# A key-value product from hi and lo parts, and state updates moved behind the output projection's residual additions

## The chip, the cores and the metric

The kernel runs on one core of a Trainium2 chip. The metric is the device time of one execution in microseconds. TensorE (PE) multiplies, VectorE (DVE), ScalarE (ACT) and GpSimd (POOL) compute on vectors, and SyncE (SP) issues nearly all DMAs. Each engine runs its own stream of instructions in order; semaphores order the streams against each other.

## The reference

One inference step of a two-layer decoder, for a prompt of 16 + 512 tokens and for 8 decode samples of one token: layer 0 mixes tokens by retention, layer 1 by a short gated convolution, each followed by a convolutional gated FFN. All 536 columns (528 prompt tokens and 8 samples) pass the weights together. The change touches the retention layer, cut here to its core (4 heads, dk = 256, dv = 512):

```python
scores = einsum('bhnd,bhmd->bhnm', q, k) * decay_mask
inner  = einsum('bhnm,bhme->bhne', scores, v)
cross  = einsum('bhnd,bhde->bhne', q, s_prev) * cross_decay
k_decay = exp(log_gamma * (L - 1 - n))
kv     = einsum('bhmd,bhme->bhde', k * k_decay, v)
s_new  = exp(log_gamma * L) * s_prev + kv
x = x + (silu(g) * groupnorm(inner + cross)) @ w_out
```

For the prompt, kv is a product over all 528 tokens, whose result is the new state of the prompt. For each of the 8 samples, kv is one outer product of its k (256) and v (512), and its state of 256 x 512 is read from HBM, multiplied by the decay, added to and written back.

## The kernel before, in words

**Layout.** Activations are feature-major: 128 features on the partitions, tokens on the free axis. Weights come from HBM in units of 128 x 1024 (512 KB). SP loads a unit into one of two raw buffers (`load`, L290 to L298). ACT rounds it to fp32r, the hi part (`split_hi`, L846 to L851), DVE subtracts that from the raw unit, the lo part (`split_lo`, L1159 to L1162), into one of four places. A product with weights is then three fp32r matmuls, hi*hi, hi*lo and lo*hi (`three`, L400). A unit is 48 matmuls of some 264 columns. A raw buffer is loaded again after both splits of the unit before last; a unit is split once the unit four places before it has been used.

**A head** of the retention layer takes 16 units: 0 to 3 for Q and K, 4 to 7 for V, 8 to 11 for the gate, 12 to 15 for the output projection. On PE (`head`, L488):
1. Q and K products (units 0, 1, then 2, 3) into PSUM banks 2 to 5 and 0, 1, 6, 7; DVE rotates Q when units 0 and 1 are done and K when units 2 and 3 are (`rotate`, L1274, four products at L1280 and two sums each).
2. V by rows of tokens (units 4 to 7, L514 to L538) into banks 2 to 5. Its first matmul waits for the four products of Q's rotation (L514), which read those banks. V is scaled from PSUM by ACT (blocks 0 and 2, L941) and DVE (blocks 1 and 3, L1331, L1333), in fp32.
3. K is transposed (L548) and scaled by the decay into `k_rows` (ACT, L957); the scores (L565); then the key-value product (L569 to L584): for two halves e of dk and four blocks j of 128 tokens, an fp32 matmul of 512 columns (L575), and for the last 16 tokens a stacked fp32r matmul (L581). The state after the first two blocks is copied out (L972) and used for the later tokens.
4. The inner product with the scores (L593 to L611), the gate (units 8 to 11), group norm and z = silu(g)*o, split into hi and lo (L1004, L1405), and the output projection (L650 to L664), whose unit pairs p = 0 to 3 DVE adds to the residual x (L1437).

**The samples' states.** ACT forms the outer product of sample b as two scaled copies of v, which a DMA has broadcast to all partitions (`outer`, L943 to L951), into one of two halves of the tile `gate`; DVE adds it to the decayed state (`update`, L1350 to L1353). A pair of copies waits for the update before last. In the order that is written out by hand, all eight stand between the splits of units 9 to 13 and the group norm: ACT L977, L980, L982, L986, L987, DVE L1359, L1372, L1376, L1386, L1387. The gate's linear part reuses the tile and waits for all eight (L1408).

**SP's queue** (L328 to L357) is in order: units 0 to 5, the decay table, eight state loads, units 6 to 10, v to HBM and its broadcast back, units 11 to 13, the prompt's kv store, eight state stores, each behind its update, units 14 and 15. After the last head, units of the FFN follow (L366). In the last head ACT and DVE also normalise each new tile of x for the FFN (L1022, L1442), and PE computes the statistic of the norm (`norm_statistic`, L443) in the midst of the FFN's second unit.

Of the kernel before, what the change touches and what calls it, by code (L numbers as in the profile page):

```python
# [36 lines left out]
P = 128  # L37
# [33 lines left out]
X_SETUP = 0  # L71
PAIR_A, PAIR_B = (1, 2), (0, 3)
# [24 lines left out]
def build(nc, io):  # L97
# [8 lines left out]
    with ctx:  # L106
# [32 lines left out]
        with ExitStack() as s2:  # L139
            with ExitStack() as s3:  # L140
                VB = sb("v_bcast", [P, NB, DV], scope=s3)
            ZRH = sb("ret_z_hi", [P, 4, N_RET], F32R, scope=s2)
            ZRL = sb("ret_z_lo", [P, 4, N_RET], F32R, scope=s2)
            S = sb("states", [P, NB, 2 * DV], scope=s2)
            O = sb("q_k_or_out", [P, 4, T], scope=s2)
            Q, K = O[:, 0:2, :], O[:, 2:4, :]
            V = sb("v_rows", [P, 5, DV], scope=s2)
            KN = sb("k_rows", [P, 4, DK], scope=s2)
            KT = sb("k_tail_stack", [P, DK], F32R, scope=s2)
            G = sb("gate", [P, 4 * N_RET], scope=s2)  # L150
            PR = sb("scores", [P, PCOL[4]], scope=s2)
            VS = sb("v_tail_stack", [P, DV], F32R, scope=s2)
# [72 lines left out]
        v_some, sel_ready = sem("v_some"), sem("sel_ready")  # L225
# [29 lines left out]
        def _(pool):  # L255
# [24 lines left out]

            pool.memset(VS[:].bitcast(F32), 0.0).then_inc(vs_zero, 1)  # L281

# [5 lines left out]
        def _(sp):  # L288
# [39 lines left out]
            def head(h, first):  # L328
                for n in range(4 if first else 0, 6):
                    in_heads(h, n)  # L330
                if first:
                    sp.wait_ge(ss_sum, 7)
                else:
                    sp.wait_ge(s_upd, NB * h)
                sp.dma_start(DEC[:], io["decay"][h]).then_inc(dec_in, 16)
                for b in range(NB):
                    if not first:
                        sp.wait_ge(s_out[b], 16 * h)
                    sp.dma_start(S[:, b, :], st_in[b, h]).then_inc(s_in[b], 16)
# [5 lines left out]
                sp.wait_ge(v_sent, 16 * h + 16)  # L345
                for half in range(2):
                    b = half * NB // 2
                    sp.dma_start(VB[:, b:b + NB // 2, :], VSCR[b:b + NB // 2, :].partition_broadcast(P)).then_inc(vb_in[half], 16)
# [4 lines left out]
                for b in range(NB):  # L353
                    sp.wait_ge(s_upd, NB * h + (b + 1))
                    sp.dma_start(st_out[b, h], S[:, b, :]).then_inc(s_out[b], 16)
                for n in range(14, 16):
                    in_heads(h, n)  # L357

            for h in range(HEADS):
                head(h, h == 0)  # L360
# [5 lines left out]
            def ffn_units(l):  # L366
                with sp.Fori(0, JF // 2) as i:
# [28 lines left out]
        def _(pe):  # L396
# [91 lines left out]
            def head(h, first, last):  # L488
# [54 lines left out]
                for j, (m0, mn) in enumerate(BLK):  # L543
                    for e in range(2):
                        at = (j % 2) * DK + e * P
                        if j == 4 and e == 0:
                            pe.wait_ge(v_some, 2 * h + 1)
# [5 lines left out]
                for j, (m0, mn) in enumerate(BLK):  # L553
                    if j == 0:
                        pe.wait_ge(v_ready, 3 * h + 2)
                        pe.wait_ge(v_some, 2 * h + 1)
                    elif j == 1:
                        pe.wait_ge(v_ready, 3 * h + 3)
                    elif j == 2:
                        pe.wait_ge(v_some, 2 * h + 2)  # L560
# [8 lines left out]
                pe.wait_ge(kn_ready, 4 * h + 4)  # L569
                for js in ((0, 1), (2, 3, 4)):  # L570
                    for e in range(2):
                        if js[0] == 2:
                            pe.wait_ge(mid_ready, 2 * h + e + 1)
                        for j in js[:2]:
                            out = mm(PS[:, 6 + e, :], KN[:, j, e * P:(e + 1) * P], V[:, j, :], start=j in (0, 2), stop=j == 1)  # L575
# [264 lines left out]
        def _(act):  # L840
# [73 lines left out]

            def head(h, first, last):
# [23 lines left out]
                for b in (0, 2):  # L939
                    act.wait_ge(v_acc, 3 * h + b + 1)  # L940
                    fn(V[:, b, :], PS[:, 2 + b, :], ACT.Copy, scale=RN[:, b:b + 1]).then_inc(v_ready, 1)  # L941

                def outer(b):  # L943

                    if b in (0, NB // 2):
                        act.wait_ge(vb_in[b // (NB // 2)], 16 * h + 16)
                    if b >= 2:
                        act.wait_ge(s_upd, 8 * h + (b - 1))
                    for e in range(2):
                        at = (b % 2) * 1024 + e * DV  # L950
                        fn(G[:, at:at + DV], VB[:, b, :], ACT.Copy, scale=KD8[:, e, b:b + 1]).then_inc(samp_kv, 1)  # L951

                act.wait_ge(dec_in, 16 * h + 16)
                act.wait_ge(knat_done, 2 * h + 1)
                for j in range(4):
                    src = PS[:, (6, 6, 7, 7)[j], (j % 2) * DK:(j % 2 + 1) * DK]
                    fn(KN[:, j, :], src, ACT.Copy, scale=DEC[:, DEC_ROW + j:DEC_ROW + j + 1]).then_inc(kn_ready, 1)  # L957
# [5 lines left out]
                act.wait_ge(vs_zero, 1)  # L963
# [5 lines left out]
                split_hi(5 + NS, U_HEAD, h)  # L969
# [3 lines left out]
                fn(OS[:], PS[:, 1, :], ACT.Copy).then_inc(os_ready, 1)  # L973
                split_hi(6 + NS, U_HEAD, h)
                if first:
                    act.wait_ge(prep_step, 12)
                outer(0)  # L977
                split_hi(7 + NS, U_HEAD, h)

                outer(1)  # L980
                for dt in range(4):
                    outer(dt + 2)  # L982
# [3 lines left out]
                outer(6)  # L986
                outer(7)  # L987
# [41 lines left out]
            for b in range(NB):  # L1029
                act.wait_ge(s_out[b], 16 * HEADS)  # L1030

            def ffn(l, norm_no):
# [3 lines left out]
                def body(i, first):  # L1036
                    split_hi(u0 + NS, 4, i)
                    if first:
                        act.wait_ge(stat_done, norm_no + 1)
                        root(3, n_in // 2, halves(R[:, c0:]), rstd)  # L1040
                    split_hi(u0 + 1 + NS, 4, i)
# [12 lines left out]
                    split_hi(u0 + 3 + NS, 4, i)  # L1054
                    for t in range(2):
# [99 lines left out]
        def _(dve):  # L1155
# [116 lines left out]

            def head(h, first, last):
# [52 lines left out]
                dve.wait_ge(v_ready, 3 * h + 1)  # L1326
# [3 lines left out]
                dve.wait_ge(v_acc, 3 * h + 2)  # L1330
                ts(V[:, 1, :], PS[:, 3, :], RN[:, 1:2], None, ALU.mult).then_inc(v_some, 1)  # L1331
                dve.wait_ge(unit_done, U_HEAD * h + (NS + 8))
                ts(V[:, 3, :], PS[:, 5, :], RN[:, 3:4], None, ALU.mult).then_inc(v_some, 1)  # L1333

                dve.wait_ge(score_done, 3 * h + 1)
                tt(PR[:, C_RET:PCOL[1]], PS[:, 2, C_RET:CUT], DEC[:, C_RET:CUT], ALU.mult).then_inc(p_ready, 1)
                dve.wait_ge(score_done, 3 * h + 2)
# [12 lines left out]
                def update(b):  # L1350
                    dve.wait_ge(samp_kv, 16 * h + (2 * b + 2))
                    at = (b % 2) * 1024
                    stt(S[:, b, :], S[:, b, :], DEC[:, DEC_STATE:DEC_STATE + 1], G[:, at:at + 1024], ALU.mult, ALU.add).then_inc(s_upd, 1)  # L1353

# [4 lines left out]
                update(0)  # L1359
                split_lo(NS + 7, U_HEAD, h)  # L1360
# [11 lines left out]
                for b in range(1, 5):  # L1372
                    update(b)
                for dt in range(1, 4):
                    channel_sum(dt)
                update(5)  # L1376
# [9 lines left out]
                update(6)  # L1386
                update(7)  # L1387
# [20 lines left out]
                dve.wait_ge(s_upd, NB * h + NB)  # L1408
# [24 lines left out]
                for p in range(4):  # L1433
# [15 lines left out]
            def ffn(l, norm_no):  # L1449
# [306 lines left out]
```

## Time and profile before

| what | value |
|---|---|
| median of 3 runs | 1459.53 us (1459.17 to 1459.82) |
| time of the profiled execution | 1459.5 us |
| its span, first to last instruction | 1457.7 us |
| granted TensorE clock, mean | 1.000 |
| HBM read, written | 149.39 MB, 21.55 MB |

The span in 40 slices of some 36 us; a digit is the busy share of a slice in tenths:

```profile
PE   9999999999999999999999999999999999999998
DVE  7785577468458855555552327444565555553222
ACT  5552273264155633333331324222343333332222
```

The heads are the first twelve to thirteen slices (a head is 121 us), the FFN of layer 0, the convolution layer and the second FFN follow. A busy engine in such a line has an instruction running; it may still be waited for by nobody. Matmuls are pipelined and their ends are modelled, so intervals between the starts of successive matmuls say what one costs.

### The profile page before, as it was taken

To read this page: it belongs to the slowest core of one execution; us is meant where nothing else is said; L and a number is where in the kernel's file an instruction comes from. 1 tells how busy PE (TensorE), PEld (TensorE's weight loads), DVE (VectorE), ACT (ScalarE), POOL (GpSimd) and SP (SyncE) were. 2 spreads that over 40 slices of the span, in tenths; PEclk is the share of its full clock that TensorE was granted. 3 is DMA by queue.
4 is the path that set the end of the run, shared out by engine and by line. 5 is a ranking of instruction groups with operands and counts; after the bars stand their busy time and mean duration, and the time that the engine had idled before them with its cause. 6 is when DMAs were issued, how large, how long until landed. Compare 5 with 4: busy or idle time off the path is not lost.

```text
span 1457.7 us, 27410 instructions
## 1 busy us (share of the span) xinstructions
PE 1451.0 (100%) x11460; PEld 1396.8 (96%) x11460; DVE 798.6 (55%) x1063; ACT 543.5 (37%) x776; POOL 3.4 (0%) x25
## 2 busy tenths in 40 slices
PE   9999999999999999999999999999999999999998
PEld 8699789879969999999999999999999999999998
DVE  7785577468458855555552327444565555553222
ACT  5552273264155633333331324222343333332222
POOL 0000000000000000000000000000000000000000
PEclk9999999999999999999999999999999999999999
DMA  8445253463444322222222222223222222223221
GB/s 300 147 187 183 102 214 118 170 228 108 177 155 184 102 93 96 86 86 96 91 90 88 100 88 87 87 89 101 89 87 98 89 86 95 92 86 99 94 87 59
DMA packets 47743, 171.91 MB, mean 118 GB/s; under 512 B 5608, under 2 KB 6248, under 8 KB 46624
## 3 DMA queue, kind: packets, MB, share of 16 engines
q1 hardware_dynamic: 47488, 170.71, 33.7%
q8 instruction: 63, 1.03, 0.3%
q14 instruction: 16, 0.13, 0.0%
q0 software_dynamic: 32, 0.03, 0.0%
q10 hardware_dynamic: 144, 0.00, 0.0%
HBM read 149.39 MB, written 21.55 MB: 117 GB/s over the span
## 4 chain that ended last, share of the span: by engine, by line
issue 100%; POOL 0%; POOLq 0%
POOLq L106 0%; POOL v_tail_stack L281 0%; POOL ident L266 0%; POOL k_tail_stack L275 0%; POOL h_tail L263 0%; POOL mean_v L259 0%; POOL ident L257 0%; POOL h_lo L262 0%; POOL h_hi L261 0%; POOL sample_ones L274 0%; POOL mean_d L258 0%; POOL scores_end_stack L277 0%; POOL late_q_decayed L276 0%; POOL sample_ones L279 0%; POOL seed L268 0%
## 5 line engine op out<-in xcount | busy, mean ns | idle before, releaser
L851 ACT ACTIVATE w_hi<-w_raw 128x1024 fp32r<-128x1024 f32 x227 | 240.0, 1059 | 669.1 <-PE ps L406 469.9
L406 PE MATMUL ps<-h_hi,w_hi 128*128 128x264 f32 (+2 forms) x2300 | 468.3, 285 | 1.5 <-DVE h_lo L1190 1.5
L406 PE MATMUL ps<-h_lo,w_hi 128*128 128x264 f32 (+2 forms) x2300 | 465.3, 284 | 0.0
L406 PE MATMUL ps<-h_hi,w_lo 128*128 128x264 f32 (+2 forms) x2300 | 465.0, 283 | 0.0
L1162 DVE TENSOR_TENSOR w_lo<-w_raw,w_hi 128x1024 fp32r<-128x1024 f32 x227 | 277.1, 1223 | 332.1 <-ACT w_hi L851 331.8
L406 PEld LDWEIGHTS ps<-h_hi,w_hi 128*128 128x128 f32 x2300 | 355.8, 188 | 2.8 <-issue 2.1
L406 PEld LDWEIGHTS ps<-h_hi,w_lo 128*128 128x128 f32 x2300 | 355.5, 188 | 0.0
L406 PEld LDWEIGHTS ps<-h_lo,w_hi 128*128 128x128 f32 x2300 | 355.2, 188 | 0.0
L700 PE MATMUL ps<-z_hi,w_hi 128*128 128x264 f32 (+1 forms) x704 | 144.6, 283 | 0.0
L700 PE MATMUL ps<-z_hi,w_lo 128*128 128x264 f32 (+1 forms) x704 | 144.6, 283 | 0.0
L700 PE MATMUL ps<-z_lo,w_hi 128*128 128x264 f32 (+1 forms) x704 | 144.5, 283 | 0.0
L700 PEld LDWEIGHTS ps<-z_lo,w_hi 128*128 128x128 f32 x704 | 109.9, 188 | 0.0
L700 PEld LDWEIGHTS ps<-z_hi,w_lo 128*128 128x128 f32 x704 | 109.8, 188 | 0.0
L700 PEld LDWEIGHTS ps<-z_hi,w_hi 128*128 128x128 f32 x704 | 109.8, 188 | 0.0
L1484 DVE TENSOR_TENSOR tmp<-ps,rms 128x524 f32<-128x524 f32 (+1 forms) x44 | 28.8, 697 | 76.1 <-PE ps L406 76.1
L1465 DVE TENSOR_TENSOR tmp<-ps,rms 128x528 f32<-128x528 f32 (+1 forms) x44 | 29.0, 701 | 68.9 <-PE ps L406 68.9
L532 PE MATMUL ps<-w_hi,h_hi 128*128 128x512 f32 x128 | 52.2, 408 | 0.0
L406 PE MATMUL ps<-ret_z_hi,w_hi 128*128 128x264 f32 x256 | 52.0, 284 | 0.0
L406 PE MATMUL ps<-ret_z_lo,w_hi 128*128 128x264 f32 x256 | 51.9, 284 | 0.0
L406 PE MATMUL ps<-ret_z_hi,w_lo 128*128 128x264 f32 x256 | 51.8, 284 | 0.0
L532 PE MATMUL ps<-w_hi,h_lo 128*128 128x512 f32 x128 | 50.5, 395 | 0.0
L532 PE MATMUL ps<-w_lo,h_hi 128*128 128x512 f32 x128 | 50.5, 394 | 0.0
(208 smaller groups left out, 1413.7 us busy)
## 6 DMA issues: line engine op xcount, KB each, us to landing
w_raw<-in_w_units_dram SPq DMA_DIRECT2D x227, 512.0 KB, 3.2
states<-in_state_ret_dram SPq DMA_DIRECT2D x32, 512.0 KB, 9.0
out_ret_s_dram<-states SPq DMA_DIRECT2D x32, 512.0 KB, 4.7
v_bcast<-v_scratch SPq DMA_DIRECT2D x8, 1024.0 KB, 5.7
x_res<-in_x_all_dram SPq DMA_DIRECT2D x8, 268.0 KB, 6.1
out_ret_p_dram<-tmp SPq DMA_DIRECT2D x4, 512.0 KB, 3.8
out_y_prompt_dram<-y_rows SPq DMA_DIRECT2D x4, 512.0 KB, 2.6
decay<-in_decay_dram SPq DMA_DIRECT2D x4, 287.0 KB, 3.9
```

The source lines that it names most:

```text
L406: out = mm(PS[:, 2 * s + half, at:at + n_col], a, b[:, lo:lo + n_col], start=first and n == 0, stop=last and n == 2)
L532: out = mm(PS[:, 2 + b, :], a, c, start=k == 0 and q == 0, stop=k == KD - 1 and q == 2)
L700: out = mm(PS[:, 2 * DOWN[t] + half, to:to + n_col], a, z[:, j, lo:lo + n_col], start=j == 0 and q == 0, stop=j == JF - 1 and q == 2)
L851: fn(WH[:, c % NS, :], RAW[:, c % NR, :], ACT.Copy).then_inc(hi_ready, 1)
L1162: tt(WL[:, c % NS, :], RAW[:, c % NR, :], WH[:, c % NS, :].bitcast(F32), ALU.subtract).then_inc(lo_ready, 1)
L1465: tt(halves(TMP[:, t, 0:n_in]), slot(PAIR_A[t], w), halves(R[:, c0:]), ALU.mult).then_inc(up_read, 1)
L1484: tt(halves(TMP[:, t, 4:n_in]), slot(PAIR_B[t], n_out // 2), halves(R[:, c0 + 4:]), ALU.mult).then_inc(gate_read, 1)
```

## The change

**Products.** `k_rows` becomes two fp32r tiles, hi and lo, and V gets a hi and a lo tile beside its fp32 one. ACT writes all four blocks of V and their hi parts and K's hi part, DVE the lo parts. Each of the eight products of a head is three fp32r matmuls in place of an fp32 one. The stacked matmuls and all other products stay.

**Outer products and updates** leave the middle of the head. In heads 1 to 3 samples 0, 1 follow pair 1 of the output projection's additions, 2, 3 follow pair 2, 4 to 7 follow pair 3. In the last head 0, 1 follow pair 0 with its norm tiles, 2, 3 pair 1, and 4 to 7 stand in the first body of the FFN, behind the root (ACT) and the reciprocal (DVE).

**SP** loads V's broadcast only when the inner product is done, since the tile that takes it now lies over V, the scores and the value stack; the next head's (or the FFN's) units 0 and 1 come ahead of the stores, 2 and 3 between them; in a head after the first, state loads 0 to 3 come ahead of units 4 and 5. POOL clears the value stack once a head, after the last update of the head before.

The diff, cut to its core:

```diff
+UPDATES = (((), (0, 1), (2, 3), (4, 5, 6, 7)), ((0, 1), (2, 3), (), ()))
...
-                VB = sb("v_bcast", [P, NB, DV], scope=s3)
+                VH = sb("v_rows_hi", [P, 4, DV], F32R, scope=s3)
+                VL = sb("v_rows_lo", [P, 4, DV], F32R, scope=s3)
...
+            with ExitStack() as s7:
+                KNH = sb("k_rows_hi", [P, 4, DK], F32R, scope=s7)
+                KNL = sb("k_rows_lo", [P, 4, DK], F32R, scope=s7)
...
-            pool.memset(VS[:].bitcast(F32), 0.0).then_inc(vs_zero, 1)
+            for h in range(HEADS):
+                if h > 0:
+                    pool.wait_ge(samp_kv, 16 * h)
+                pool.memset(VS[:].bitcast(F32), 0.0).then_inc(vs_zero, 1)
...
+            def head(h, first, last):
+                if not first:
+                    for b in range(4):
+                        load_state(b)
+                for n in range(4, 6):
                     in_heads(h, n)
...
+                for b in range(0 if first else 4, NB):
+                    load_state(b)
                 for n in range(6, 11):
                     in_heads(h, n)
...
                 sp.wait_ge(kv_ready, h + 1)
                 sp.dma_start(kv_dst[h], KV).then_inc(kv_sent, 16)
-                for b in range(NB):
-                    sp.wait_ge(s_upd, NB * h + (b + 1))
-                    sp.dma_start(st_out[b, h], S[:, b, :]).then_inc(s_out[b], 16)
+                sp.wait_ge(v_sent, 16 * h + 16)
+                sp.wait_ge(inner_done, 4 * h + 4)
+                for half in range(2):
+                    b = half * NB // 2
+                    sp.dma_start(VB[:, b:b + NB // 2, :], VSCR[b:b + NB // 2, :].partition_broadcast(P)).then_inc(vb_in[half], 16)
                 for n in range(14, 16):
                     in_heads(h, n)
+                for n in range(2):
+                    next_unit(h, n)
+                for p in range(4):
+                    for b in UPDATES[last][p]:
+                        store_state(h, b)
+                    if p in (1, 2):
+                        next_unit(h, 1 + p)
+                if last:
+                    ffn_in_unit(0, 1, 0)
+                    for b in range(4, NB):
+                        store_state(h, b)
...
-                pe.wait_ge(kn_ready, 4 * h + 4)
...
+                            pe.wait_ge(kn_lo, 4 * h + 2 * e + 2)
+                            pe.wait_ge(v_lo, 4 * h + 4)
                         for j in js[:2]:
-                            out = mm(PS[:, 6 + e, :], KN[:, j, e * P:(e + 1) * P], V[:, j, :], start=j in (0, 2), stop=j == 1)
+                            kh, kl = KNH[:, j, e * P:(e + 1) * P], KNL[:, j, e * P:(e + 1) * P]
+                            for q, (k, v) in enumerate(((kh, VH), (kh, VL), (kl, VH))):
+                                out = mm(PS[:, 6 + e, :], k, v[:, j, :], start=j in (0, 2) and q == 0, stop=j == 1 and q == 2)
...
                 for p in range(4):
                     if not (last and p == 3):
                         split_hi(12 + p + NS, U_HEAD, h)
+                    for b in UPDATES[last][p]:
+                        outer(h, b)
                     if last:
...
                         root(3, n_in // 2, halves(R[:, c0:]), rstd)
+                    if first and l == 0:
+                        for b in range(4, NB):
+                            outer(HEADS - 1, b)
...
-                ts(V[:, 1, :], PS[:, 3, :], RN[:, 1:2], None, ALU.mult).then_inc(v_some, 1)
...
+                for b in range(4):
...
+                    tt(VL[:, b, :], V[:, b, :], VH[:, b, :].bitcast(F32), ALU.subtract).then_inc(v_lo, 1)
...
                     if last:
                         for k in (2 * p, 2 * p + 1):
                             norm_tile(k, 1, C_RET, N_RET, D_FFN)
+                    for b in UPDATES[last][p]:
+                        update(h, b)
...
                         dve.wait_ge(r_ready, norm_no + 1)
+                        if l == 0:
+                            for b in range(4, NB):
+                                update(HEADS - 1, b)
```

ACT's order in the middle changes with it: the split of unit 9 now follows the copies of the middle state (L972), and DVE's split of unit 11 follows the kv sum (L1371).

## Rows read from the trace of the kernel before

**Rows 1.** The page, busy us (share of the span) xinstructions

```profile
PE 1451.0 (100%) x11460; PEld 1396.8 (96%) x11460; DVE 798.6 (55%) x1063; ACT 543.5 (37%) x776; POOL 3.4 (0%) x25
```

**Rows 2.** The waits, TensorE: waited for, us in total, times, longest us

```profile
PE ps L406 <- DVE h_lo L1190: 1.5, 3, 0.7
```

**Rows 3.** Timeline, TensorE, third head: start us, us to last end, instruction, count

```profile
302.31 0.40 PE L532 MATMUL ps<-w_hi,h_lo 128*128 128x512 f32 x1
302.55 0.39 PE L532 MATMUL ps<-w_lo,h_hi 128*128 128x512 f32 x1
302.77 1.25 PE L548 MATMUL ps<-ident,q_k_or_out 128*128 128x128 f32 x10
...
306.86 5.42 PE L575 MATMUL ps<-v_rows,k_rows 128*128 128x512 f32 x12
311.71 0.79 PE L581 MATMUL ps<-v_tail_stack,k_tail_stack 96*128 96x512 f32 x1
312.35 1.88 PE L575 MATMUL ps<-v_rows,k_rows 128*128 128x512 f32 x4
...
314.30 0.80 PE L603 MATMUL ps<-scores,v_rows 128*128 128x248 f32 x4
```

**Rows 4.** Timeline, ScalarE, third head, in brackets the idle time before it

```profile
301.58 0.69 ACT L941 ACTIVATE v_rows<-ps,rms_rows 128x512 f32<-128x512 f32 x1 [2.10 <-PE ps L532]
303.91 1.57 ACT L957 ACTIVATE k_rows<-ps,decay 128x256 f32<-128x256 f32 x4 [1.64 <-PE ps L548]
...
312.52 1.33 ACT L951 ACTIVATE gate<-v_bcast,dec_k 128x512 f32<-128x512 f32 x2
```

**Rows 5.** Groups by line, whole span: xcount, busy us, mean ns, idle before

```profile
L851 ACT ACTIVATE w_hi<-w_raw 128x1024 fp32r<-128x1024 f32 x227 | 240.0, 1059 | 669.1 <-PE ps L406 469.9
L1162 DVE TENSOR_TENSOR w_lo<-w_raw,w_hi 128x1024 fp32r<-128x1024 f32 x227 | 277.1, 1223 | 332.1 <-ACT w_hi L851 331.8
L1353 DVE SCALAR_TENSOR_TENSOR states<-states,decay,gate 128x1024 f32<-128x1024 f32 x32 | 40.3, 1280 | 2.6 <-ACT gate L951 2.6
```

**Rows 6.** Timeline, third head, where the output projection starts

```profile
348.80 0.70 DVE L1405 TENSOR_TENSOR ret_z_lo<-q_k_or_out,ret_z_hi 128x528 fp32r<-128x528 f32 x1
...
349.94 0.40 PE L406 MATMUL ps<-ret_z_hi,w_hi 128*128 128x264 f32 x2
```

**Rows 7.** Timeline, last head: rotation of Q, start of the value product

```profile
387.35 0.70 DVE L1280 SCALAR_TENSOR_TENSOR q_k_or_out<-ps,cos_r 128x528 f32<-128x528 f32 x1
...
389.19 0.70 DVE L1280 SCALAR_TENSOR_TENSOR tmp<-ps,cos_r 128x528 f32<-128x528 f32 x1
...
396.76 0.39 PE L532 MATMUL ps<-w_hi,h_hi 128*128 128x512 f32 x1
```

**Rows 8.** State loads; landings of those issued at 376.8 and 380.9; weight loads

```profile
376.83 4.49 SPq L339 DMA_DIRECT2D states<-in_state_ret_dram  x8
...
DMA to landing us min/median/max: 5.7/5.7/5.7
...
DMA to landing us min/median/max: 11.2/11.2/11.2
...
w_raw<-in_w_units_dram SPq DMA_DIRECT2D x227, 512.0 KB, 3.2
```

**Rows 9.** Timeline, last head into the FFN

```profile
492.23 1.22 DVE L1162 TENSOR_TENSOR w_lo<-w_raw,w_hi 128x1024 fp32r<-128x1024 f32 x1
...
494.33 0.41 PE L406 MATMUL ps<-h_hi,w_hi 128*128 128x264 f32 x2
...
499.69 0.71 DVE L1175 TENSOR_TENSOR tmp<-tmp 128x528 f32<-128x528 f32 x1
...
501.63 1.05 PE L439 MATMUL ps<-tmp,mean_d 128*128 128x264 f32 x4
```

**Rows 10.** Stretches at the start: us, TensorE busy (x), clock, DMA share, GB/s

```profile
1.30:4.30 3.00, 3.00 (x14) 1.00 0.74 230
4.40:5.40 1.00, 1.00 (x11) 1.00 0.71 168
```

More of the change, by code:

```diff
@@ L326, in _, with ffn_in_unit, next_unit, store_state @@
             sp.dma_start(CF[:], io["ffn_consts"]).then_inc(ffn_in, 16)
-            def head(h, first):
-                for n in range(4 if first else 0, 6):
+            def ffn_in_unit(l, i, n):
+                load(U_FFN_IN[l] + 4 * i + n)
+            def next_unit(h, n):
+                if h < HEADS - 1:
+                    in_heads(h + 1, n)
+                else:
+                    ffn_in_unit(0, 0, n)
+            def store_state(h, b):
+                sp.wait_ge(s_upd, NB * h + (b + 1))
+                sp.dma_start(st_out[b, h], S[:, b, :]).then_inc(s_out[b], 16)
+            def head(h, first, last):
+                def load_state(b):
+                    if not first:
+                        sp.wait_ge(s_out[b], 16 * h)
+                    sp.dma_start(S[:, b, :], st_in[b, h]).then_inc(s_in[b], 16)
+                if not first:
+                    for b in range(4):
+                        load_state(b)
+                for n in range(4, 6):
                     in_heads(h, n)
@@ L344, in head @@
                 sp.dma_start(VSCR, V[16:24, 4, :]).then_inc(v_sent, 16)
[L345 to L348, printed above, removed]
                 for n in range(11, 14):
@@ L352, in head @@
                 sp.dma_start(kv_dst[h], KV).then_inc(kv_sent, 16)
[L353 to L355 removed]
+                sp.wait_ge(v_sent, 16 * h + 16)
[3 more added lines that the diff above has]
+                    sp.dma_start(VB[:, b:b + NB // 2, :], VSCR[b:b + NB // 2, :].partition_broadcast(P)).then_inc(vb_in[half], 16)
                 for n in range(14, 16):
                     in_heads(h, n)
+                for n in range(2):
[9 more added lines that the diff above has]
+                        store_state(h, b)
             for h in range(HEADS):
[L360 removed]
+                head(h, h == 0, h == HEADS - 1)
             for l in range(2):
@@ L366, in ffn_units @@
             def ffn_units(l):
-                with sp.Fori(0, JF // 2) as i:
+                if l == 1:
+                    for n in range(4):
+                        ffn_in_unit(l, 0, n)
+                for n in range(1 if l == 0 else 0, 4):
+                    ffn_in_unit(l, 1, n)
+                with sp.Fori(2, JF // 2) as i:
                     for n in range(4):
@@ L913, in _, with outer @@
             fn(RN[:], PS[:, 3, 300:305], ACT.Sqrt, bias=EPST[:]).then_inc(rows_rstd, 2)
+            def outer(h, b):
+                if b == 0:
+                    act.wait_ge(z_mul, 8 * h + 8)
+                if b in (0, NB // 2):
+                    act.wait_ge(vb_in[b // (NB // 2)], 16 * h + 16)
+                if b >= 2:
+                    act.wait_ge(s_upd, 8 * h + (b - 1))
+                for e in range(2):
+                    at = (b % 2) * 1024 + e * DV
+                    fn(G[:, at:at + DV], VB[:, b, :], ACT.Copy, scale=KD8[:, e, b:b + 1]).then_inc(samp_kv, 1)
             def head(h, first, last):
@@ L938, in head @@
                 fn(VT, PS[:, 0, 0:P], ACT.Copy, scale=RN[:, 4:5]).then_inc(v_ready, 1)
-                for b in (0, 2):
-                    act.wait_ge(v_acc, 3 * h + b + 1)
-                    fn(V[:, b, :], PS[:, 2 + b, :], ACT.Copy, scale=RN[:, b:b + 1]).then_inc(v_ready, 1)
[L943 to L951, printed above, removed]
+                for b in range(4):
+                    if b < 3:
+                        act.wait_ge(v_acc, 3 * h + b + 1)
+                    else:
+                        act.wait_ge(unit_done, U_HEAD * h + (NS + 8))
+                    fn(V[:, b, :], PS[:, 2 + b, :], ACT.Copy, scale=RN[:, b:b + 1]).then_inc(v_ready, 1)
+                    fn(VH[:, b, :], PS[:, 2 + b, :], ACT.Copy, scale=RN[:, b:b + 1]).then_inc(v_hi, 1)
                 act.wait_ge(dec_in, 16 * h + 16)
+                if first:
+                    act.wait_ge(prep_step, 12)
                 act.wait_ge(knat_done, 2 * h + 1)
@@ L973, in head @@
                 fn(OS[:], PS[:, 1, :], ACT.Copy).then_inc(os_ready, 1)
+                split_hi(5 + NS, U_HEAD, h)
                 split_hi(6 + NS, U_HEAD, h)
-                if first:
-                    act.wait_ge(prep_step, 12)
-                outer(0)
                 split_hi(7 + NS, U_HEAD, h)
-                outer(1)
                 for dt in range(4):
-                    outer(dt + 2)
                     act.wait_ge(inner_done, 4 * h + (dt + 1))
@@ L1054, in body @@
                     split_hi(u0 + 3 + NS, 4, i)
+                    if first and l == 0:
+                        for b in range(NB):
+                            act.wait_ge(s_out[b], 16 * HEADS)
                     for t in range(2):
@@ L1271, in first_scale, with update @@
                         tt(t[:, e, c:], t[:, e, c:], R[:, c:], ALU.mult).then_inc(qk_scaled, 1)
+            def update(h, b):
+                dve.wait_ge(samp_kv, 16 * h + (2 * b + 2))
+                at = (b % 2) * 1024
+                stt(S[:, b, :], S[:, b, :], DEC[:, DEC_STATE:DEC_STATE + 1], G[:, at:at + 1024], ALU.mult, ALU.add).then_inc(s_upd, 1)
             def head(h, first, last):
@@ L1371, in head @@
                 tt(KV, PS[:, 6:8, :].rearrange("p e v -> p (e v)"), KM, ALU.add).then_inc(kv_ready, 1)
-                for b in range(1, 5):
-                    update(b)
+                split_lo(NS + 7, U_HEAD, h)
                 for dt in range(1, 4):
                     channel_sum(dt)
-                update(5)
                 dve.wait_ge(gstat_done, 2 * h + 1)
```

62 lines of the change are left out of this document (26 added, 36 removed).

## The prediction

> **What bounds the kernel now.** I read the busy line first: TensorE is busy for 1451.0 of 1457.7 us, VectorE for 798.6, ScalarE for 543.5 [rows 1]. Then the waits: beside one before the very first matmuls, the only wait of TensorE is 1.5 us at the start [rows 2]. So the kernel is a TensorE stream with no holes. A change can gain only what it takes out of that stream, and every wait that it opens is lost in full. The averages of the other engines don't say whether one opens; that is decided in the stages, followed below with the third head (297 to 397 us) as pattern.
>
> **The products.** Two fp32r matmuls of 512 columns start 0.23 us apart (302.31, 302.55, 302.77). The old key-value block runs from 306.86 to 314.30: 16 fp32 records and two stacked ones [rows 3]. That is 7.44 us; with 0.23 for each stacked one, an fp32 record costs (7.44 - 0.46)/16 = 0.436, a product two of them, 0.87. The new product is three fp32r matmuls, 0.69. A head has eight products: 24 x 0.23 + 0.46 = 5.98, and with some 0.1 for the change of operand 6.1. Gain: 1.3 us a head, 5.3 us in all. Bounds: nothing, if fp32r ran no faster here, and 5.8 without the 0.1.
>
> **The split of V and K** is covered. ScalarE now makes eight copies of 512 columns where it made two (0.69 each, some 0.6 apart), each pair as its block finishes every 1.4 us. The last pair starts at 303.0 and ends at 304.3; the four key copies, 1.57 us, end at 305.8 instead of 305.5 [rows 4]. VectorE loses two copies and gets four differences of V (0.7 each, like the residuals of [rows 6]) and four of K (0.5, an estimate from 256 of 512 columns): V's last rest is there at 305.1, K's first two at 306.0, the others, behind one score product, at 307.2. TensorE has ten transposes and the scores until 306.86 and takes the second pair at 308.25, so nothing waits; the nearest margin is 0.9 us. The score products come about 0.5 us later and hold up only the copies of the middle state, needed at 309.6 and there at 309.2. If that cover were gone, 0.5 us a head would be lost. The clearing of the value stack on POOL is off every path: POOL is idle and the stack is next used some 40 us later, with the next head's V.
>
> **Updates out of the middle.** In the third head the first rest of z is finished at 349.50, TensorE starts the output projection at 349.94 [rows 6]: 0.4 us of room. The 1.3 us gained would mostly be lost there if nothing moved. Without six updates (1.28 us each) and eight outer pairs (1.33 us) [rows 4, 5] ahead of it, this chain ends about 3 us earlier. The gain survives, and TensorE starts at 348.6.
>
> **Updates behind the residual additions, heads 1 to 3.** TensorE takes 5.85 us a weight unit (46.8 us from 349.94 to 396.76 for eight) [rows 6, 7]. So projection pair 1 ends at 360.3, and the value product of the next head should start at 395.4. Call the next head's weight units N0 to N5. SyncE issues in order: N2 stands behind the stores of states 0 and 1, N3 behind 2 and 3; N4 and N5, until now loaded before any state, stand behind stores 4 to 7 **and** four state loads. The chain:
> - 360.5 N1 is split on ScalarE (1.06), two outer pairs (2.6), second update (1.3): 365.5.
> - Store, N2 issued 366.0, landed 369.3 (3.2) [rows 8], split on ScalarE 370.4, two pairs 373.0, fourth update 374.3.
> - Store, N3 issued 374.8, landed 378.1, ScalarE 379.2, VectorE (1.22) 380.5.
> - Updates 4 to 7: 1.3 each, plus a wait for the buffer of two (a pair needs the update before last): 386.0.
> - Store, four state loads half a microsecond apart (eight in 4.49), N4 issued at 388.4, N5 at 388.8.
> - Landing: the first state load of the old burst took 5.7 us, the eighth, issued 4.0 later, 11.2: they land in turn, (380.9 + 11.2 - 376.8 - 5.7)/7 = 1.37 apart [rows 8]. The first of four at 386.4 + 3.2 = 389.6, so N4 at 395.1 and N5 at 396.5.
> - N5 on ScalarE 397.6, on VectorE 398.8; both are written before the rotation of Q, whose fourth product comes 2.54 us later [rows 7]: 401.4.
> TensorE may not overwrite the banks before that: 401.4 - 395.4 = **6.0 us of stall**. Before, that product was there at 389.89, 6.9 us early. It happens at three boundaries: 18.0 us. Bounds: 2.4 each if N4 and N5 do not queue behind the states (below), 7.5 if the burst starts as slowly as the old one (5.7 instead of 3.2).
>
> **Last head.** There the same engines also normalise the new tiles. Times from the start of the projection (before: 494.33 - 23.4 = 470.9). VectorE: additions of pair 0 to 10.3, split to 11.5, norm of two tiles (held back by the outer pairs on ScalarE) to 15.8, two updates to 18.1, additions of pair 1 to 19.4. TensorE wants these at 17.5: stall 1.9. Split 20.6, norm 23.4, updates 25.8, additions of pair 2 27.0; wanted at 25.3: stall 1.7. FFN unit 2 now stands behind store 3: issued 26.3, landed 29.5, split on both engines 31.9. From there the old kernel took from 493.45 to 500.40, 6.95 us, to the last sum of squares; its statistic ran at 501.63, 1.2 us later [rows 9]. New: 38.9, wanted at 501.63 - 470.9 + 3.6 = 34.3, stall 4.6. Sum **8.2 us**. Bounds: 3.7 (four updates, 4.9, less the 1.2 of room) and 10. The last four updates, behind the reciprocal, end at about 51; the banks that they hold back are wanted at 56. They and the FFN loads behind their stores cost nothing; without that cover they would cost up to 5.
>
> **Clock.** The only start of TensorE from rest in this trace: 14 matmuls of 128 columns in 3.0 us, later 11 in 1.0 [rows 10], though the column of the granted clock says 1.00 for both; the spacing is that of 1.2 and then 2.4 GHz. Those 14 cost about 1.4 us more than later ones. Whether a hole of 6 us brings this back no row shows: nothing at the least, 2.8 at the most (twice as many). I take 1.4 for each of the three, because the row after a rest is the nearest: 4.2 us.
> The Trainium skill's page "TensorE: Matmul & The Clock Gate" (Part 1) says that the array falls to half clock when it has been idle. By that rule the three stalls cost the 4.2 us; without it the sum is 1480.4.
>
> **Sum**, against the profiled execution's 1459.5 us (span 1457.7, 1.8 around it; the median of the runs is 1459.53, the same): 1459.5 - 5.3 + 18.0 + 8.2 + 4.2 = **1484.6 us**. Measurement tells some 0.2%, 2.9 us, from no change.
>
> **Rivals.**
> - No drop of the clock, all else as above: 1480.4. For it: a hole is not the start of a kernel. Chance 0.2.
> - The weight loads overtake the states. N4 and N5 would land at 391.6 and 392.0, the rotation's fourth product be there at 397.8, a stall of 2.4 each and no drop of the clock: 1459.5 - 5.3 + 7.2 + 8.2 = 1469.6. Against it: the old state loads land one after another. Chance 0.1.
>   The Trainium skill's page "DMA: Bandwidth & Descriptors" (Queues, rings and completion order) states that completion isn't first-in first-out per issuing engine, which is this rival's rule.
> - Faster: all moved updates are hidden, and the gain stays: 1454.2. The one mechanism is the slack of the rotation of Q, 6.9 us before. It decides at N5's landing: by 390.4 (395.4 less the 5.0 of splits and rotation) TensorE would see nothing. For it: VectorE is only half busy. Against: the chain needs 388.8 for the mere issue, and the last head has 1.2 us of room for 4.9 us of work. Chance 0.1.
> - The products don't get faster (three fp32r cost what two records of fp32 do): 1489.9. Against: [rows 3]. Chance 0.03.
>
> **Chances and range.** My forecast has 0.5; 0.07 is left for what I haven't seen, most of it slower. Range 1465 to 1494: the lower end takes in the overtaking loads with a cheap last head, the upper three stalls of 7.5 and the dearer clock. Faster 0.1, the same 0.04, slower 0.86.
>
> **What would show it.** Waits of TensorE before the first 512-column product of heads 2 to 4, about 6 us, ended by the rotation (L1280), its VectorE idle until a split that ScalarE started on a landing weight; matmuls after it at twice the spacing; three smaller waits in the last projection and at the first FFN statistic. Key-value records 0.23 us apart, the block 6.1 us long. z's rests earlier than the projection by 2 us. If no wait stands before the value product, the chain on SyncE is wrong; if it is 2.4, the queueing is; if the key-value block still takes 7.4 us, the gain is.

## The result, and the profile after

The changed kernel takes **1498.93 us** (median of 4 runs, 1498.53 to 1499.47) beside 1459.55 us of the kernel before (1459.17 to 1459.82): a ratio of 1.0271, 95% interval 1.0258 to 1.0283. That is 39.4 us slower where 25.1 were forecast, and above the range. The profiled execution has a span of 1497.5 us. Of the executions reported below, one of the ten of experiment 7 took 5309.54 us at a granted clock of 1.0; nothing on record explains it, and no ratio here contains it.

First the page of the changed kernel, busy time by engine and the row of slices of TensorE (PEclk is its granted clock, in tenths):

```profile
PE 1455.8 (97%) x11492; PEld 1409.4 (94%) x11492; DVE 809.5 (54%) x1087; ACT 557.5 (37%) x800; POOL 5.0 (0%) x28
...
PE   9999799799979989999999999999999999999998
...
PEclk9999899999999999999999999999999999999999
```

The full stream of [rows 1] now has places below 9: three between the heads and one in the last head. Then the waits of TensorE (waited for: us in total, times, longest us):

```profile
PE ps L574 <- DVE tmp L1332: 25.6, 3, 10.1
PE ps L481 <- DVE tmp L1222: 4.5, 1, 4.5
PE ps L448 <- DVE x_res L1489: 3.2, 2, 1.8
...
PE ps L448 <- DVE h_lo L1215: 1.1, 1, 1.1
```

[Rows 2] held 1.5 us there. L574 is the value product of heads 2 to 4, L1332 the rotation of Q, L481 the first FFN statistic, L1489 the residual additions of the last head, L1215 the lo part of a tile that is normalised for the FFN.

**The products** in the third head (timeline of TensorE: start us, us, instruction, count):

```profile
326.88 0.50 PE L616 MATMUL ps<-v_rows_hi,k_rows_hi 128*128 128x512 f32 x1
327.21 0.39 PE L616 MATMUL ps<-v_rows_lo,k_rows_hi 128*128 128x512 f32 x1
...
333.05 0.58 PE L644 MATMUL ps<-scores,v_rows 128*128 128x248 f32 x2
```

The block takes 333.05 - 326.88 = 6.17 us instead of the 7.44 of [rows 3], one product every 0.23. By the starts of the stages the four heads save 1.26 to 1.27 each, 5.05 in all.

**The split** is there in time. ScalarE (first row) and VectorE in the same head:

```profile
324.15 1.57 ACT L1006 ACTIVATE k_rows_hi<-ps,decay 128x256 fp32r<-128x256 f32 x4
```

```profile
325.02 0.88 DVE L1391 SCALAR_TENSOR_TENSOR k_rows_lo<-ps,decay,k_rows_hi 128x256 fp32r<-128x256 f32 x2
...
326.14 0.87 DVE L1391 SCALAR_TENSOR_TENSOR k_rows_lo<-ps,decay,k_rows_hi 128x256 fp32r<-128x256 f32 x2
```

The first pair of rests is finished at 325.9, a microsecond ahead of the product; the second at 327.0, wanted some 1.4 us after 326.88. **The chain of z** gained what was forecast: its first rest ends at 366.5 and the output projection starts at 368.69, 2.2 us of room instead of the 0.4 of [rows 6]:

```profile
365.79 0.70 DVE L1458 TENSOR_TENSOR ret_z_lo<-q_k_or_out,ret_z_hi 128x528 fp32r<-128x528 f32 x1
```

**The holes.** The queue of SyncE between the second and third head (projection from 238.82), behind the stores of states 0 and 1 at 254.35 and 255.55; then landings of single weight loads, of N2 (255.99), N3 (265.27) and N4 (280.08) here, and of N3 one boundary earlier:

```profile
255.99 0.40 SPq L307 DMA_DIRECT2D w_raw<-in_w_units_dram  x1
263.61 1.56 SPq L348 DMA_DIRECT2D out_ret_s_dram<-states  x2
265.27 0.41 SPq L307 DMA_DIRECT2D w_raw<-in_w_units_dram  x1
273.32 4.25 SPq L348 DMA_DIRECT2D out_ret_s_dram<-states  x4
277.62 2.37 SPq L354 DMA_DIRECT2D states<-in_state_ret_dram  x4
280.08 0.98 SPq L307 DMA_DIRECT2D w_raw<-in_w_units_dram  x2
...
DMA to landing us min/median/max: 3.9/3.9/3.9
...
DMA to landing us min/median/max: 4.3/4.3/4.3
...
DMA to landing us min/median/max: 7.4/7.4/7.4
...
DMA to landing us min/median/max: 5.4/5.4/5.4
```

What waited for it, on ScalarE, VectorE and TensorE:

```profile
287.57 1.06 ACT L892 ACTIVATE w_hi<-w_raw 128x1024 fp32r<-128x1024 f32 x1 [11.67 <-DMA w_raw<-in_w_units_dram]
```

```profile
288.66 2.50 DVE L1209 TENSOR_TENSOR w_lo<-w_raw,w_hi 128x1024 fp32r<-128x1024 f32 x2 [11.44 <-ACT w_hi L892]
291.07 0.70 DVE L1332 SCALAR_TENSOR_TENSOR q_k_or_out<-ps,cos_r 128x528 f32<-128x528 f32 x1
...
292.92 0.70 DVE L1332 SCALAR_TENSOR_TENSOR tmp<-ps,cos_r 128x528 f32<-128x528 f32 x1
```

```profile
285.40 0.41 PE L448 MATMUL ps<-h_hi,w_lo 128*128 128x268 f32 x2
293.67 0.80 PE L574 MATMUL ps<-w_hi,h_hi 128*128 128x512 f32 x1 [7.86 <-DVE tmp L1332]
294.26 0.63 PE L574 MATMUL ps<-w_hi,h_lo 128*128 128x512 f32 x1
294.69 0.63 PE L574 MATMUL ps<-w_lo,h_hi 128*128 128x512 f32 x1
```

ScalarE stood idle for 11.7 us (the number in brackets) until N4 had landed, VectorE for 11.4 until ScalarE had split it: neither was short of time. TensorE starts the value product 10.2, 8.0 and 7.9 us late at the three boundaries, by the starts of the stages.

**The clock.** Behind the hole the products stand 0.43 us apart and not 0.23. Four stretches, two in the wait and two behind it (us, TensorE busy (x), weight loads, VectorE, ScalarE, POOL, granted clock, DMA share, GB/s):

```profile
285.30:291.00 5.70, 0.51 (x5) 0.29 (x3) 2.29 (x2) 2.11 (x2) 0.00 (x0) 1.00 1.03 411
291.00:293.60 2.60, 0.00 (x0) 0.00 (x0) 2.60 (x5) 0.00 (x0) 0.00 (x0) 0.51 1.01 400
...
293.70:297.70 4.00, 4.00 (x10) 3.13 (x11) 3.93 (x7) 0.00 (x0) 0.00 (x0) 0.50 0.01 4
298.10:302.10 4.00, 4.00 (x31) 2.65 (x29) 3.10 (x7) 2.56 (x4) 0.00 (x0) 1.00 0.13 20
```

The clock is at its lower level, 1.2 GHz, already at the end of the wait; it makes the three value products longer by 2.15, 2.03 and 2.02 us. The same rows show the DMA engines full (share 1.03 and 1.01, 411 and 400 GB/s) all through the wait: N4 and N5 landed in the midst of a burst, four state loads ahead of them and four behind.

**The last head**: the projection becomes 3.56 us longer, and from the FFN's first product to steady work 8.55 more are lost, 1.1 and 4.5 of them waits (above), the rest, 2.9, at half clock.

| term, us | forecast | measured |
|---|---|---|
| products | -5.3 | -5.05 |
| three holes | 18.0 | 26.1 |
| last head, waits | 8.2 | 9.2 |
| clock | 4.2 | 9.1 |
| sum | 25.1 | 39.35 |

### The profile page after: what moved, and what is told of

It reads as the page before. It is cut to its first block, busy times and chain, and to the rows that moved or that the text cites. A ratio compares the mean times of both kernels' runs of the same rounds, so it can differ in the third digit from the quotient of the medians.

```text
span 1497.5 us, 27488 instructions
## 1 busy us (share of the span) xinstructions
PE 1455.8 (97%) x11492; PEld 1409.4 (94%) x11492; DVE 809.5 (54%) x1087; ACT 557.5 (37%) x800; POOL 5.0 (0%) x28
## 3 DMA queue, kind: packets, MB, share of 16 engines
q8 instruction: 63, 1.03, 0.3%
## 4 chain that ended last, share of the span: by engine, by line
issue 73%; PE 19%; DMA 3%; DVE 3%; ACT 1%; SPq 1%; POOLq 0%; POOL 0%; ACTq 0%
PE ps L448 8%; PE ps L574 5%; DMA w_raw<-in_w_units_dram 3%; DVE states L1323 2%; PE ps L616 1%; DVE w_lo L1209 1%; PE ps L647 1%; ACT w_hi L892 1%; PE ps L602 1%; PE ps L644 1%; PE ps L649 1%; PE ps L481 0%; PE ps L544 0%; PE ps L553 0%; ACT gate L966 0%
## 5 line engine op out<-in xcount | busy, mean ns | idle before, releaser
L574 PE MATMUL ps<-w_hi,h_hi 128*128 128x512 f32 x128 | 55.2, 432 | 25.6 <-DVE tmp L1332 25.6
L574 PEld LDWEIGHTS ps<-w_hi,h_hi 128*128 128x128 f32 x128 | 25.6, 200 | 34.7 <-DVE tmp L1332 26.3
L574 PE MATMUL ps<-w_hi,h_lo 128*128 128x512 f32 x128 | 52.6, 411 | 0.0
L574 PE MATMUL ps<-w_lo,h_hi 128*128 128x512 f32 x128 | 52.6, 411 | 0.0
```

What stands on the lines that cost most here:

```text
L574: out = mm(PS[:, 2 + b, :], a, c, start=k == 0 and q == 0, stop=k == KD - 1 and q == 2)
```

## The experiments

The theory after the result: **the order of SyncE's queue** makes the holes (weight loads stand behind state stores, which stand behind updates), and each hole costs clock on top. Its rivals: the updates' own work on ScalarE and VectorE, or slow transfers.

**1. Weight loads ahead of the stores, heads 1 to 3.**

```diff
                 for p in range(4):
+                    if not last:
+                        next_unit(h, 2 + p)
                     for b in UPDATES[last][p]:
                         store_state(h, b)
-                    if p in (1, 2):
+                    if last and p in (1, 2):
                         next_unit(h, 1 + p)
...
                 if not first:
                     for b in range(4):
                         load_state(b)
-                for n in range(4, 6):
-                    in_heads(h, n)
+                else:
+                    for n in range(4, 6):
+                        in_heads(h, n)
```

> Edit: in heads 1 to 3 SyncE issues each weight load of the next head (N2 to N5) ahead of the state stores that it stood behind, and N4 and N5 ahead of the four state loads; no work of any engine and no byte changes, and the last head stays as it is. Theory Q (the loads stand in SyncE's order behind stores that wait for updates): the three holes before the value products (10.2, 8.0, 7.9 us, sum 26.1) go, and with them the slow value matmuls behind them (6.2 us in all): 1498.9 - 32.3 = 1466.6 us, with the last head's stalls unchanged. Rival W (the updates' own work on ScalarE and VectorE is too much at that place): the rotation of Q stays late by the updates' 1.3 us each, holes of 3 us or more stay, 1476 us or more. Rival B (the transfers are slow because stores and loads share the DMA engines): holes of 2 to 4 us stay.

Measured: 1467.44 us (1466.92 to 1467.65), ratio to before 1.0054 (1.0037 to 1.0071). The waits of TensorE hold no value product any more:

```profile
PE ps L484 <- DVE tmp L1225: 4.5, 1, 4.5
PE ps L451 <- DVE x_res L1492: 3.1, 2, 1.8
```

VectorE at the same place in front of the fourth head, whose value product starts at 393.19:

```profile
376.15 1.29 DVE L1326 SCALAR_TENSOR_TENSOR states<-states,decay,gate 128x1024 f32<-128x1024 f32 x1
...
382.63 1.23 DVE L1212 TENSOR_TENSOR w_lo<-w_raw,w_hi 128x1024 fp32r<-128x1024 f32 x1 [4.05 <-ACT w_hi L895]
383.77 0.70 DVE L1335 SCALAR_TENSOR_TENSOR q_k_or_out<-ps,cos_r 128x528 f32<-128x528 f32 x1
...
385.62 0.70 DVE L1335 SCALAR_TENSOR_TENSOR tmp<-ps,cos_r 128x528 f32<-128x528 f32 x1
```

All eight updates are done at 377.4 and the rotation is 6.9 us early, as it was before the change. No instruction of ScalarE, VectorE or TensorE differs: 31.5 us are the order of one queue (and the clock that the holes cost). The rival of the work falls for these heads. That of slow transfers falls as a cause of its own: issued early, N4 and N5 land 3.3 and 3.4 us after their issue (from 366.57 and 372.40). But where these loads come late, transfers that share the full DMA engines are a part of the hole: N4 took 4.9 us behind the stores (experiment 2), and 7.4 behind four state loads as well (the changed kernel).

**2. Only N4 and N5 ahead of the state loads**

```diff
-                if not first:
-                    for b in range(4):
-                        load_state(b)
                 for n in range(4, 6):
                     in_heads(h, n)
+                if not first:
+                    for b in range(4):
+                        load_state(b)
```

> Edit: in heads 1 to 3 only N4 and N5 are issued ahead of the four state loads of the next head; they still stand behind the eight stores, as N2 and N3 do. Theory Q: N4 is issued some 2 us earlier and lands 4 us behind its issue instead of 7.4, so each hole shrinks by 5 us, from 8 to about 3 (the first to 5): 1498.9 - 15 = 1484 us, and up to 6 less (1478) if TensorE's clock doesn't fall after so short a hole. Rival W (work of the updates): the order of these loads decides nothing, 1499. Rival B (shared DMA engines): N4 and N5 still take 7 us behind the stores, 1495 or more.

**3. Only N2 and N3 ahead of the stores**

```diff
                 for p in range(4):
+                    if not last and p < 2:
+                        next_unit(h, 2 + p)
                     for b in UPDATES[last][p]:
                         store_state(h, b)
-                    if p in (1, 2):
+                    if last and p in (1, 2):
                         next_unit(h, 1 + p)
```

> Edit: in heads 1 to 3 only N2 and N3 are issued ahead of the stores; N4 and N5 stay behind the stores and the four state loads. Theory: the updates then end 7.3 us earlier (31.1 us behind the projection's start, by the trace of the run with all four ahead, instead of 38.4), so N4 and N5 land that much earlier and the holes shrink from 8 to about 1, too short for the clock to fall: 1467.4 + 3 x 1 = 1470.4 us. If the clock falls after such a hole too, 2 us more each, 1476. Rival: the queueing behind the state loads is the larger part, holes of 3 us or more stay, 1480.

Measured: 1484.84 us (1482.26 to 1487.1) with N4 and N5 moved, 1470.80 (1470.56 to 1473.37) with N2 and N3 moved. The waits before the value product, the first row of the one, the second of the other:

```profile
PE ps L574 <- DVE tmp L1332: 11.4, 3, 5.2
```

```profile
PE ps L576 <- DVE tmp L1334: 4.1, 3, 1.6
```

So the holes are the sum of two queueings: N2 and N3 behind the first stores delay the updates themselves (28.1 us of the loss), N4 and N5 behind the four state loads delay the rotation (14.1); either repair alone leaves a part. They sum to more than the 31.5 of experiment 1 because a hole opens only where the rotation's 6.9 us of slack are used up: what either repair gives beyond that point is slack again. N4 and N5 landed 4.9 and 5.8 us after their issue in front of the state loads (experiment 2, issued from 272.79), 8.2 and 9.0 behind them (experiment 3, from 383.16):

```profile
DMA to landing us min/median/max: 4.9/5.3/5.8
```

```profile
DMA to landing us min/median/max: 8.2/8.6/9.0
```

These two runs also show **the clock against the length of a hole**. Where the wait was 3.0 us (experiment 2), then where it was 1.2 (experiment 3, value product from 275.96):

```profile
280.70:283.30 2.60, 0.29 (x3) 0.07 (x1) 2.60 (x5) 0.00 (x0) 0.00 (x0) 1.00 1.01 412
283.30:290.10 6.80, 6.12 (x14) 4.79 (x15) 6.19 (x12) 0.44 (x1) 0.00 (x0) 0.50 0.87 341
```

```profile
276.00:279.00 3.00, 3.00 (x13) 2.48 (x14) 2.97 (x5) 0.00 (x0) 0.00 (x0) 1.00 0.02 5
```

A wait of 3.0 us cost more clock than one of 8: the value product behind it was 2.9 us longer, 2.5 at the first boundary (wait 5.2), 1.4 at the third (wait 3.2). Behind the waits of 1.2 to 1.6 the value product took 0.1 us more than before. All these are prices of single executions, and they vary: the four executions of experiment 2 took 1482.26, 1484.56, 1485.13 (the profiled one) and 1487.10 us, with mean granted clocks of 0.995, 0.993, 0.990 and 0.990.

**4. The last head's updates in the first FFN body**, all eight behind the reciprocal:

```diff
-UPDATES = (((), (0, 1), (2, 3), (4, 5, 6, 7)), ((0, 1), (2, 3), (), ()))
+UPDATES = (((), (0, 1), (2, 3), (4, 5, 6, 7)), ((), (), (), ()))
...
-                    ffn_in_unit(0, 1, 0)
-                    for b in range(4, NB):
+                    for n in range(3):
+                        ffn_in_unit(0, 1, n)
+                    for b in range(NB):
                         store_state(h, b)
...
-                        for b in range(4, NB):
+                        for b in range(NB):
                             outer(HEADS - 1, b)
```

(and `range(NB)` in VectorE's loop too, `range(3, 4)` for the first layer's units behind it).

> Edit: in the last head all eight updates stand behind the reciprocal of the first FFN body, none in the output projection; the FFN weight loads stand ahead of their stores. Heads 1 to 3 as in the changed kernel. Theory: the last head's loss goes, which the trace puts at 3.6 us in the projection, 5 more up to the FFN statistic and some 2.7 behind it at the slow clock, 11.2 in all: 1498.9 - 11.2 = 1487.7 us, if eight updates (some 11 us) behind the reciprocal are covered as four were. Rival: those eight hold back the up-projection's banks and the split of FFN units, and give back 5 us or more: 1493 or more.

Measured: 1488.48 us (1486.58 to 1489.32), 10.4 less than the changed kernel. Only the three holes are left beside 0.3 us in the FFN:

```profile
PE ps L575 <- DVE tmp L1333: 25.4, 3, 10.3
```

Eight updates behind the reciprocal are covered, as the forecast said of four.

**5. Both repairs.**

> Edit: both at once, the weight loads ahead of the stores in heads 1 to 3, and the last head's eight updates in the first FFN body. Theory: the two repairs add up, since they lie at different places: 1467.4 - 10.4 = 1457.0 us by the medians; by the traces, 5.05 us of the products kept less the 0.6 that the FFN body took and no hole anywhere, 1455.2. So 1455 to 1457, some 3 us under the kernel before. Rival: with the holes gone something else comes late (the transfers of states and FFN weights meet in the last head), 1459 or more.

Measured: **1455.25 us** (1455.17 to 1455.62), ratio to before 0.9972 (0.9962 to 0.9983): 4.2 us under the kernel before, and the fastest of all. The longest wait of TensorE left is one at the kernel's start, and no other is longer than 0.3:

```profile
PE ps L499 <- POOL mean_d L264: 1.1, 1, 1.1
```

**6. The fp32 product again**, in the changed kernel and in the one with both repairs:

```diff
-                            kh, kl = KNH[:, j, e * P:(e + 1) * P], KNL[:, j, e * P:(e + 1) * P]
-                            for q, (k, v) in enumerate(((kh, VH), (kh, VL), (kl, VH))):
-                                out = mm(PS[:, 6 + e, :], k, v[:, j, :], start=j in (0, 2) and q == 0, stop=j == 1 and q == 2)
+                            out = mm(PS[:, 6 + e, :], KNH[:, j, e * P:(e + 1) * P], V[:, j, :], start=j in (0, 2), stop=j == 1)
```

(`KNH` is an fp32 tile here, so that K isn't rounded.)

> Edit: the key-value product again in fp32 from the unsplit V and K (two fp32 products of 512 columns where the changed kernel has six fp32r ones), all else, the copies and differences of the split too, as in the changed kernel. If the 5.05 us that the key-value blocks are shorter in the trace are the product's whole worth, and they count in full: 1498.9 + 5.05 = 1504.0 us, blocks of 7.4 us. Rival: part of the gain was given back at the holes (a hole is measured from the output projection, which then starts later, so it should not change), under 1502.

> Edit: the kernel with both repairs, but the key-value product in fp32 from the unsplit V and K. It leaves the moved updates without the faster products. Theory: the products are worth their 5.05 us here as in the trace, so 5 us more than with both repairs, about 1461 us; the move alone brings nothing where TensorE has no hole. Rival: part of that gain is lost elsewhere when the stream has no holes, under 1459.

Measured: 1505.65 us (1504.92 to 1506.6), 6.7 more than the changed kernel, and 1460.30 (1460.02 to 1461.0), 5.05 more than with both repairs; the ratio of the latter to before is 1.0007 (0.9998 to 1.0016). So the products are worth 5.05 us where the stream has no holes, and the move by itself nothing (0.9 us more than before, inside the interval). In the changed kernel 1.7 us more came on top, which was not expected. In the traces (6.1 us apart) it is the holes, 28.1 us in all instead of 26.1, with 0.7 less lost from the last projection on: N2 in front of the third head landed 5.7 us after its issue, where it took 3.9 in the changed kernel.

```profile
DMA to landing us min/median/max: 5.7/5.7/5.7
```

That part of the products' gain is given back at the holes is excluded. The block of the third head with both repairs and fp32 takes 7.43 us (307.04 to 314.47), as in [rows 3].

**7. Weight loads first in the last head too**, its updates left in the projection: the edit of experiment 1 with `(4 if not last else 2)` units in all four heads.

> Edit: the weight loads ahead of the stores in all four heads (in the last one FFN units 2 and 3 ahead of the stores of states 0 and 1, 2 and 3), the last head's updates left in the output projection. It tells apart what of the last head's 10.4 us is the order of the loads and what the updates' work. Theory: the waits for the additions (1.8 and 1.3) are work and stay; FFN unit 2 comes 4 us earlier, the wait before the FFN statistic falls from 4.5 to 1 or 2, and the clock stays: 1467.4 - 5.7 = 1461.7 us. If the order were all of it: 1457. If the work were all of it: 1467.

Measured: 1459.13 us (nine of ten from 1458.94 to 1459.67), 8.3 less than experiment 1, ratio to before 0.9998 (0.9989 to 1.0008). The forecast of 1461.7 was too high: in the profiled execution the wait before the statistic fell from 4.5 to 0.5, not to 1 or 2, and of the two waits for the additions one is left. But TensorE spent 3.4 us of that execution at half clock just before (last section), which may have taken up a part of both waits. By the mean clock (0.998) that holds for two of the nine; the other seven (1.000) took no less, and none of them has a trace.

```profile
PE ps L451 <- DVE x_res L1492: 1.8, 1, 1.8
...
PE ps L484 <- DVE tmp L1225: 0.5, 1, 0.5
```

Of the last head's 12.2 us (1467.44 to 1455.25), 8.3 are the order of the queue and the clock behind it, and 3.9 the work of four updates among the additions and norms.

## Why the prediction was right in direction and wrong in size

- **Products**: right, 5.05 for 5.3. The 0.1 us for the change of operand is what the block shows (6.17).
- **Split of V and K, chain of z**: right. Nothing waits, z has 2.2 us of room. What the products alone would have done, with the updates left in the middle, was not tried: V's hi and lo tiles lie where its broadcast rows were.
- **The mechanism of the holes**: right in every link. Relative to the projection's start, forecast and measured at the second boundary: N2 issued 17.4 and 17.2, N3 issued 26.2 and 26.45, last update 37.4 and 38.4, N4 issued 39.8 and 41.3, landed 46.5 and 48.7, the rotation's fourth product 52.8 and 54.8. **The failing term is the landing of a load behind stores.** I took 3.2 us, the median of the group, which is made of loads that are alone; N2 took 3.9, N3 4.3 and the first state load 4.4, and at the first boundary N3 took 5.4. Each of these stands in series with the next, so 0.7 to 2.2 us each became most of the 2.0, 1.9 and 4.2 by which the holes exceed 6.0; half a microsecond at the second boundary is SyncE's, which took 2.9 us and not 2.4 from the last update to N4's issue. The DMA engines are full while these loads are on the way (share 1.02 from 256 to 258 us and from 266 to 268, with two stores issued just ahead of each load). In the burst the forecast's 1.37 us from one landing to the next held (282.0 to 287.5 for four). The upper bound of 7.5 was derived from the first load of a burst only; the loads in the middle of the chain had no bound of their own.
- **The clock**: the second failing term. The sum had 1.4 us for each of three holes. A hole cost 2.0 to 2.2, and the wait before the FFN statistic, which the sum held free of this, 2.9 more: 9.1 for 4.2. The forecast's 1.4 came from the kernel's start, where the slow matmuls cover 3.0 us [rows 10]; behind a hole they cover some 4. By the rows themselves it should have been 1.5 (half of 3.0) to 1.7 (3.0 less 14/11), which closes only a part.
  The Trainium skill's page "TensorE: Matmul & The Clock Gate" (Part 1) says that the array falls to half clock when it has been idle. The trace agrees: 1.00 falls to 0.50 in each of the three holes and in the wait of 4.5 us.
- **Last head**: waits 9.2 for 8.2, right in place. The forecast gave 3.6 to work and 4.6 to the late weight; experiment 7 bears this out (3.9 of work), with the clock as part of what the late weight cost.
- **Rivals**: loads that overtake the states did not come: in this trace the four state loads land before N4 (the last at 286.2, N4 at 287.5), N4 before N5 (288.8). The Trainium skill's page "DMA: Bandwidth & Descriptors" (Queues, rings and completion order) states that completion isn't first-in first-out per issuing engine; no exception from the order shows among these six loads. The faster case (1454.2) is what the kernel with both repairs reaches, 1455.25. The forecast named the point where it decides, N5's landing, and it does: the same updates at the same place cost nothing once the weights land early.
- **Range**: its upper end took the holes at 7.5 and the dearer clock together: 1459.5 - 5.3 + 22.5 + 8.2 + 8.4 = 1493.3. The bound of a hole was mis-summed: with the burst as slow as the old one it is 6.0 + 5.7 - 3.2 = 8.5, and the end 1496.3. The result lies above that too: holes 26.1 for 25.5, clock 9.1 for 8.4, the last head's waits 9.2 for the 8.2 of the sum, and products that gave 0.25 less.

## What to carry to other kernels

Before moving work that ends in a store, write down the issuing queue's order at the new place: a load behind a store waits for everything that the store waits for. Here the same move cost 39 us or gained 4, and only the order of DMA issues and the last head's place differ. Issue a load when its buffer is free, not after the stores of the same step; and count, for a bubble in TensorE's stream, the slow clock behind it, which here was 1.4 to 2.9 us for each wait of 3 us or more in the profiled executions.

## What was not expected of the hardware

The cost of the clock doesn't grow with the wait. In the wait of 7.9 us the clock fell while TensorE still stood, and 2.0 us were lost behind it; in the one of 3.0 it fell at the end, stayed low for 6.8 us, and 2.9 were lost. A wait of 1.8 us in the last projection was followed by no slow stretch in the profiled execution of experiment 1 and by one in that of experiment 7, with the same instructions around it (the first row experiment 1, then 7):

```profile
485.60:490.00 4.40, 4.33 (x36) 4.36 (x36) 4.36 (x6) 2.54 (x5) 0.00 (x0) 1.00 0.23 88
```

```profile
485.40:486.50 1.10, 1.05 (x8) 1.08 (x9) 1.10 (x2) 1.10 (x3) 0.00 (x0) 1.00 0.82 339
486.50:489.90 3.40, 3.40 (x18) 3.40 (x17) 3.37 (x5) 2.36 (x4) 0.00 (x0) 0.50 0.46 155
```

In the second the clock fell 1.1 us after TensorE had started again. It isn't the kernel that decides: by the mean clocks only two of experiment 7's nine executions had such a stretch, and their times (1459.21 and 1459.34 us) lie among those of the others (1458.94 to 1459.67), so that it cost nothing that can be seen. What decides no run here shows.
